# First loads one stage ahead, raw rope rows, two-pass norms and a late residual add in an eight-stage decoder layer

## The chip, the cores and the metric

The kernel runs on one core of a Trainium2 chip. The metric is the device time of one launch in microseconds (us). One execution was also taken by the hardware profiler; its times count from the start of its span.

## What is computed

One layer on 1024 tokens of width 1024, all in float32: a mixing sublayer and a retrieval sublayer, each followed by a layer norm of `alpha * x + result`.

```python
h = x @ w_in                                        # 58 blocks of 128 columns, and 12 columns "ba"
y_a = dilated_attention(rope(q_a), rope(k_a), v_a)  # 12 heads x 64, 3 patterns (window, dilation)
qkv = silu(causal_depthwise_conv(qkv_b))            # width 4
beta = sigmoid(beta_in)
g = -exp(A_log) * softplus(a_in + dt_bias)
y_b = rmsnorm(gated_delta_rule(q, k, v, g, beta)) * silu(gate_b)  # 6 heads x 128, chunks of 64
merged = gate0 * (y_a @ w_branch_attn) + gate1 * (y_b @ w_branch_delta)
x1 = layer_norm(ALPHA * x + merged @ w_out)
# PEER: 8 heads, product keys over 128 x 128 experts, top 16
s = (x1 @ w_query) against sub_keys;  experts, gate = top-k and softmax of s
act = gelu(x1 . expert_down[experts])
out = layer_norm(ALPHA * x1 + sum(gate * act * expert_up[experts]))
```

## The kernel before

The program is eight stages, one after the other, each a function with its own tiles, its own semaphores and one block of engine programs. Tile names begin with the letter of the stage:

- **p**, `stage_project` (L85): `x @ w_in`. Each of 58 weight blocks is loaded, rounded to a high part by ScalarE (ACT) and its rest taken by VectorE (DVE); TensorE (PE) multiplies high by high, high by low and low by high, so a float32 product is three matmuls (L244). The blocks come in pairs, and SyncE (SP) stores each result to `hT` in DRAM. After the last pair, 64 products of 12 columns give `psb` (L250), which goes to DRAM as `ba`.
- **a**, `stage_attention` (L255): the attention in 6 tiles of two heads. SP loads the raw q and k rows of a tile and their halves swapped (`load`, L339 and L342, 10 DMAs); POOL (GpSimd) turns them with cos and sin (L309), adds, and splits the sum into high and low parts (L313 to L316); SP copies these into the stacked operands (`restack`, L349, 12 DMAs) and the V columns (`columns`, L352). At the start PE transposes V (L495), and DVE copies it out (L445). `ahead` (L366) is SP's program for the next tile.
- **d**, `stage_deltanet` (L558): 16 chunks of the delta rule in sequence. Its start turns `ba` into beta, g and their cumulated exponentials.
- **m**, `stage_merge` (L1054): two branch products and their gates. **o**, `stage_out_norm` (L1158): the output product, 8 token tiles, each with a norm: DVE takes statistics and `(z - mean) * rstd` (L1272), POOL multiplies by the gain (L1226) and adds the bias (L1228), PE transposes the result for the next stages.
- **s**, `stage_scores` (L1348): query products. **r**, `stage_down_and_route` (L1473): 128 blocks of `x1 @ down` for 6 of the 8 token tiles, while DVE chooses experts; rows of the other two token tiles ("gathered") are fetched by POOL with indirect DMAs and multiplied on DVE.
- **e**, `stage_up` (L1946): in 32 rounds of 4 chunks, PE accumulates `C @ up` into PSUM (L2180), DVE adds each bank to `y` (L2115), prepares the low parts of the next round (L2103, L2105) and accumulates 8 gathered rows a round, `y += row * coef` (L2130), which POOL fetches (L2068). POOL also weighs the activations (L2074). At the start x1 is loaded into `y` (L2030) and taken times ALPHA. The last round brings the final norm: statistics (L1991 to L1996), `norm` (L2001) and, on POOL for all but the last tile, the gain (L2008) and the bias (L2010).

Each engine works through its own program in order and waits on semaphores. Between two stages stand barriers of all engines and the raising of the next stage's semaphores:

```python
    for s in held.values():
        nc.gpsimd.sem_inc(s, START)
    held |= {name: nc.alloc_semaphore(f"{prefix}_{name}") for name in landed.split()}
    nc.all_engine_barrier()
    yield held.__getitem__
    nc.clear_and_free_semaphores(list(held.values()))
    nc.all_engine_barrier()
```

So no load of a stage is issued before the stage ahead of it has ended on all engines and its last store has landed.

## Time and profile before

| | us |
|---|---|
| median of 3 runs | 4306.57 (4306.22 to 4308.96) |
| the profiled execution | 4310.81 |
| its span | 4309.0 |
| PE busy | 3957.7 (92% of the span) |
| DVE busy | 2586.9 (60%) |
| POOL busy | 1702.3 (40%) |
| ACT busy | 1367.3 (32%) |

The stages by their first and last matmul, and the time without a matmul ahead of each:

| stage | first and last matmul, us | no matmul ahead of it, us |
|---|---|---|
| p | 10.06 to 666.13 | |
| a | 694.99 to 965.64 | 28.9 |
| d | 985.46 to 1434.44 | 19.8 |
| m | 1449.32 to 1589.42 | 14.9 |
| o | 1603.22 to 1719.12 | 13.8 |
| s | 1729.42 to 1940.96 | 10.3 |
| r | 1959.97 to 3189.29 | 19.0 |
| e | 3208.27 to 4276.29 | 19.0 |
| end of the span | 4309.0 | 32.7 |

PE, DVE, ACT and POOL are the compute engines; SPq is SyncE issuing DMAs. The granted clock of PE is given as a share of its full speed of 2.4 GHz: 1.00 is full speed, 0.50 is 1.2 GHz. A busy time is the sum of an engine's instructions in a stretch, and what an engine waits for is inferred from the semaphores.

### The profile page before, as it was taken

The numbers are of one execution on the slowest core, as the hardware profiler recorded it, in microseconds if no ns is written. First come the engines' busy times: TensorE is split into PE (matmuls) and PEld (weight loads), VectorE is DVE, ScalarE is ACT, GpSimd is POOL, SyncE is SP. The second block draws the span as 40 slices with busy tenths as digits, with TensorE's granted clock in tenths as the row PEclk, the third lists the DMA queues.
The fourth block names the chain that finished last, engine by engine and source line by source line (L and its number), as shares of the span: only waits on it lengthen the run. The fifth ranks groups of instructions, "written<-read, shape, count | busy, mean of one in ns | idle before, by whom it ended". The sixth has DMA issues, their size and how long they took to land. (4 is left out here: it accounts for less than half of the span.)

```text
span 4309.0 us, 61280 instructions
## 1 busy us (share of the span) xinstructions
PE 3957.7 (92%) x21744; PEld 3573.4 (83%) x21744; DVE 2586.9 (60%) x5114; ACT 1367.3 (32%) x2139; POOL 1702.3 (40%) x1159
## 2 busy tenths in 40 slices
PE   9999994996888788998999999999988999999996
PEld 7888884886888666998999999999976888888885
DVE  2154102554555334116777888886648888898888
ACT  2133221652222211112472644635512222222220
POOL 0000003624444004000727656566626555555556
PEclk9999996997999899999999999999999999999998
DMA  3223224642222322223549779698888888888884
GB/s 132 97 88 106 94 86 129 160 109 71 76 75 84 138 95 94 88 68 129 136 139 318 231 227 299 201 331 278 262 315 289 289 291 290 285 290 298 280 289 185
DMA packets 390923, 801.82 MB, mean 186 GB/s; under 512 B 65265, under 2 KB 204401, under 8 KB 389745
## 3 DMA queue, kind: packets, MB, share of 16 engines
q1 hardware_dynamic: 280176, 531.25, 36.9%
q0 software_dynamic: 110592, 268.62, 19.9%
q8 instruction: 85, 1.39, 0.1%
q14 instruction: 70, 0.57, 0.0%
HBM read 623.40 MB, written 154.32 MB: 180 GB/s over the span
## 5 line engine op out<-in xcount | busy, mean ns | idle before, releaser
L1935 PE MATMUL r_psd<-x1h,r_dh 128*128 128x384 f32 x2048 | 700.9, 342 | 19.0 <-DVE r_dl L1733 19.0
L1935 PE MATMUL r_psd<-x1l,r_dh 128*128 128x384 f32 x2048 | 688.4, 336 | 0.0
L1935 PE MATMUL r_psd<-x1h,r_dl 128*128 128x384 f32 x2048 | 688.3, 336 | 0.0
L2180 PE MATMUL e_psy<-e_uh,e_Ch 128*128 128x512 f32 x1536 | 600.1, 391 | 36.3 <-DVE e_Cl L2105 31.9
L2180 PE MATMUL e_psy<-e_ul,e_Ch 128*128 128x512 f32 x1536 | 599.5, 390 | 0.0
L2180 PE MATMUL e_psy<-e_uh,e_Cl 128*128 128x512 f32 x1536 | 599.4, 390 | 0.0
L1708 POOL DMA_INDIRECT W<-r_put,r_place x256 | 426.7, 1667 | 405.6 <-DVEq L1882 319.0
L2074 POOL TENSOR_TENSOR e_araw<-e_araw,e_W 128x768 f32<-128x768 f32 x128 | 258.9, 2023 | 401.4 <-DMA e_W<-W 400.5
L1935 PEld LDWEIGHTS r_psd<-x1h,r_dh 128*128 128x128 f32 x2048 | 388.3, 190 | 19.8 <-DVE r_dl L1733 19.8
L1699 POOL DMA_INDIRECT r_rows<-in_down_rows,ids x256 | 262.7, 1026 | 358.8 <-DVE coef L1750 242.8
L2130 DVE SCALAR_TENSOR_TENSOR e_y<-e_rows,coef,e_y 128x1024 f32<-128x1024 f32 x256 | 384.5, 1503 | 15.0 <-DMA e_rows<-in_up,ids 14.9
L1935 PEld LDWEIGHTS r_psd<-x1l,r_dh 128*128 128x128 f32 x2048 | 388.3, 190 | 0.0
L1935 PEld LDWEIGHTS r_psd<-x1h,r_dl 128*128 128x128 f32 x2048 | 387.4, 189 | 0.0
L2052 ACT CAST e_uh<-e_uraw 128x1024 fp32r<-128x1024 f32 x128 | 134.8, 1053 | 789.8 <-DMA e_uraw<-in_up 495.8
L244 PE MATMUL p_ps<-p_xh,p_wh 128*128 128x512 f32 x928 | 362.0, 390 | 10.3 <-DVE p_wl L198 10.1
L2180 PEld LDWEIGHTS e_psy<-e_uh,e_Ch 128*128 128x128 f32 x1536 | 289.7, 189 | 97.8 <-DVE e_Cl L2105 32.7
L244 PE MATMUL p_ps<-p_xl,p_wh 128*128 128x512 f32 x928 | 361.6, 390 | 0.0
L244 PE MATMUL p_ps<-p_xh,p_wl 128*128 128x512 f32 x928 | 361.5, 390 | 0.0
L2068 POOL DMA_INDIRECT e_rows<-in_up,ids x256 | 331.2, 1294 | 59.1 <-issue 45.2
L2180 PEld LDWEIGHTS e_psy<-e_uh,e_Cl 128*128 128x128 f32 x1536 | 289.5, 188 | 60.5
L2180 PEld LDWEIGHTS e_psy<-e_ul,e_Ch 128*128 128x128 f32 x1536 | 289.7, 189 | 60.1
L1750 DVE CUSTOM_DVE_ANT_0 r_rows<-r_rows,r_psx 128x1024 f32<-128x1024 f32 x256 | 301.2, 1214 | 42.5 <-DMA r_rows<-in_down_rows,ids 37.1
(326 smaller groups left out, 7338.3 us busy)
## 6 DMA issues: line engine op xcount, KB each, us to landing
r_draw<-in_down SPq DMA_DIRECT2D x128, 512.0 KB, 5.3
e_uraw<-in_up SPq DMA_DIRECT2D x128, 512.0 KB, 6.2
act<-r_act SPq DMA_DIRECT2D x128, 384.0 KB, 5.0
e_araw<-act SPq DMA_DIRECT2D x128, 384.0 KB, 3.2
e_W<-W SPq DMA_DIRECT2D x128, 384.0 KB, 5.0
...
```

The lines of the kernel that those rows point to most:

```text
L244: ins = nc.tensor.matmul(ps[u][:, h * HALF:(h + 1) * HALF], a[u][:, k, :], b[:, k, h * HALF:(h + 1) * HALF], start=(k == 0 and n == 0), st ...
L1699: nc.gpsimd.indirect_dma_start(out=rows[u][:], out_offset=None, in_=g.down_rows, in_offset=bass.IndirectOffsetOnAxis(ap=g.ids[:, n, k % P: ...
L1708: nc.gpsimd.indirect_dma_start(out=cells, out_offset=bass.IndirectOffsetOnAxis(ap=place[:, n, e:e + 1], axis=0), in_=put[:, n, e:e + 1], i ...
L1750: nc.vector.tensor_tensor_reduce(out=rows[u][:], in0=rows[u][:], in1=psx[:], scale=1.0, scalar=0.0, op0=ALU.mult, op1=ALU.add, accum_out=d ...
L1935: ins = nc.tensor.matmul(psd[n][:, h, 0:HD], a[c % DEEP][:, k, :], b[:, k, h * HD:(h + 1) * HD], start=(k == 0 and m == 0), stop=(k == KD ...
L2052: nc.scalar.copy(uh[s][:], uraw[n][:]).then_inc(sem("u_hi"), 1)
L2068: nc.gpsimd.indirect_dma_start(out=rows[u][:], out_offset=None, in_=g.up.rearrange("j p d -> (j p) d"), in_offset=bass.IndirectOffsetOnAxi ...
L2074: nc.gpsimd.tensor_tensor(araw[n][:], araw[n][:], Wt[n][:], ALU.mult).then_inc(sem("weighted"), 1)
L2130: nc.vector.scalar_tensor_tensor(o, rows[u][:], scale, o, ALU.mult, ALU.add).then_inc(sem("acc"), 1)
L2180: ins = nc.tensor.matmul(bank[:], a[s][:, t * P:(t + 1) * P], v[s][:, h * HALF:(h + 1) * HALF], start=(q == 0 and m == 0), stop=(q == G - ...
```

## The change

- The semaphores of a stage are allocated and raised by POOL in the stage ahead (`raise_to_start`); between stages only the block's own end and one clear are left. Tiles that both stages see (`hand`, `out_w`, `branch_w`, `front_in`, `rope_in`, `rope_out`, `stack0`) take the first loads of the next stage, which SP issues in the stage ahead: after the last use of the buffer, and before that stage's last stores.
- In p, PE does the 12-column products after its first block product; the gate factors of d are worked out in p by ACT, DVE and PE and stay on chip. POOL turns and splits tile 0's q and k in p, and SP loads V, cos, sin, raw q and k and restacks tile 0 in p.
- In a, the sum of q or k is written over the raw rows after the high part is taken; so SP's `ahead` waits for the split, and no longer for the additions alone, before it loads the next raw rows.
- In o and e, the norm is two passes on DVE, `(z - mean) * gain` and `* rstd + bias`; POOL does the power alone. o has four weight buffers where it had two.
- In e, x1 is added late, one token tile every third round from round 3 (`add_x`); the first addition of a bank and the first two gathered rows write `y`. The first and last of the 32 rounds accumulate no rows, the second 10, the one before the last 12, the others 8 or 9. The final norm is all on DVE, and the last tile goes out in two halves.

The diff, cut to its core:

```diff
-def stage_semaphores(nc, prefix, names, landed=""):
-
-    held = {name: nc.alloc_semaphore(f"{prefix}_{name}") for name in names.split()}
-    for s in held.values():
...
+def raise_to_start(nc, sems, raised=None):
+
+    for s in sems:
         nc.gpsimd.sem_inc(s, START)
-    held |= {name: nc.alloc_semaphore(f"{prefix}_{name}") for name in landed.split()}
-    nc.all_engine_barrier()
-    yield held.__getitem__
-    nc.clear_and_free_semaphores(list(held.values()))
-    nc.all_engine_barrier()
+    if raised is not None:
+        nc.gpsimd.sem_inc(raised, 1)
 
 
...
+            table, ld_v, ld_q = g.next["ld_table"], g.next["ld_v"], g.next["ld_q"]
+            split, stacked = g.next["split"], g.next["stacked0"]
+            for i in range(att + 1, att + 17):
+                m = i - att - 1
+                pair(i)
+                if m < 6:
+                    sp.dma_start(g.vT_s[:, m, :], g.hT[2 * AT + m]).then_inc(ld_v, 16)
+                elif m < 8:
+                    sp.dma_start((g.cos_s, g.sin_s)[m - 6], (g.cos, g.sin)[m - 6]).then_inc(table, 16)
+                elif m < 12:
+                    n = m - 8
+                    block_of = g.hT[n // 2 * AT]
+                    if n % 2 == 0:
+                        sp.dma_start(g.rope_in[n][:], block_of).then_inc(ld_q, 16)
+                    else:
+                        for r in range(4):
+                            sp.dma_start(g.rope_in[n][rows[r], :], block_of[rows[r ^ 1], :]).then_inc(ld_q, 16)
+                elif m >= 14:
+                    h = m - 14
+                    sp.wait_ge(split, START + 2)
+                    for n, parts in enumerate(((0, 1), (2, 2), (3, 3))):
+                        for half, part in enumerate(parts):
+                            sp.dma_start(g.stack0[h][n][half * AD:(half + 1) * AD, :].bitcast(F32),
+                                         g.rope_out[part][h * AD:(h + 1) * AD, :].bitcast(F32)).then_inc(stacked, 16)
+            with sp.Fori(att + 17, pairs - 1) as i:
...
+            products(0, 0, first=True)
+            pe.wait_ge(ld_c, START + 96)
             for t in range(TT):
                 for k in range(KD):
                     ins = nc.tensor.matmul(psb[:, t * 2 * DH:(t + 1) * 2 * DH], x[:, k, t * P:(t + 1) * P],
                                            wba[:, k, :], start=(k == 0), stop=(k == KD - 1))
             ins.then_inc(ba_done, 1)
+            products(0, 1)
+            with pe.Fori(1, 4) as i:
+                for u in range(2):
+                    products(i, u)
+            pe.wait_ge(sem("g"), START + 1)
...
             def ahead(j, par, more=True):
 
 
+                sp.wait_ge(split, START + 4 * j + (2 * par + 4))
                 if more:
-                    sp.wait_ge(rope_done, START + 8 * j + (4 * par + 8))
                     load(2 * j + (par + 2))
-                sp.wait_ge(split, START + 4 * j + (2 * par + 4))
                 if par:
...
             ahead(AT // 2 - 1, 0, more=False)
+            for n in range(3):
+                src = g.hT[N_ATT + n * DH:N_ATT + (n + 1) * DH, :, 0:P]
+                sp.dma_start(g.front_in[n], src.rearrange("n p t -> p n t")).then_inc(g.next[f"ld_raw{n}"], 16)
             for kb in range(0, TT, 2):
...
             load_gate(0)
+            sp.wait_ge(sem("raised"), START + 1)
+            for u in range(2):
+                sp.dma_start(g.branch_w[u][:], g.w_branch[u]).then_inc(g.next[f"ld_w{u}"], 16)
+            for b in range(2):
+                sp.dma_start(g.branch_gate[:, b, :], g.hT[N_IN - N_BR + b * KD]).then_inc(g.next["ld_g0"], 16)
             sp.wait_ge(sem("none"), START + 1)
...
+            for n in range(3):
+                sp.wait_ge(sem(f"front{n}"), START + NC)
+                sp.dma_start(g.hand[n][:], g.y[n]).then_inc(g.next[f"ld_y{n}"], 16)
             sp.wait_ge(sem("y_out"), START + 2 * NC)
...
+                sp.dma_start(gates[1][:, b, :], g.hT[N_IN - N_BR + b * KD + 1]).then_inc(sem("ld_g1"), 16)
+            sp.wait_ge(sem("y_lo"), START + NK)
+            sp.wait_ge(sem("raised"), START + 1)
+            for k in range(4):
+                sp.dma_start(g.out_w[k][:], g.w_out[k * P:(k + 1) * P, :]).then_inc(g.next[f"ld_w{k}"], 16)
+            sp.dma_start(g.hand[2][:], g.x[0:P, :]).then_inc(g.next["ld_x"], 16)
             with sp.Fori(0, KD // 2 - 1) as i:
...
+                dve.wait_ge(sem("ld_c"), START + 32)
+                nc.vector.scalar_tensor_tensor(z[u][:], z[u][:], mv[:, 0:1], gain[:], ALU.subtract, ALU.mult).then_inc(sem("normed"), 1)
+                dve.wait_ge(sem("normed"), START + c + 1)
                 dve.wait_ge(sem("rstd"), START + c + 1)
-                nc.vector.tensor_scalar(z[u][:], z[u][:], mv[:, 0:1], rstd[:, 0:1], ALU.subtract, ALU.mult).then_inc(sem("normed"), 1)
+                nc.vector.scalar_tensor_tensor(z[u][:], z[u][:], rstd[:, 0:1], bias[:], ALU.mult, ALU.add).then_inc(sem("x1"), 1)
...
+            sp.wait_ge(sem("raised"), START + 1)
+            for c in (2, 0, 1):
+                if c < 2:
+                    sp.wait_ge(sem("w_lo"), START + N - 1 + c)
+                sp.dma_start(g.hand_kt[c], g.down[c]).then_inc(g.next[f"ld_d{c}"], 16)
...
+                    elif c + 2 + DEEP == PK:
+                        sp.wait_ge(sem("raised"), START + 1)
+                        sp.wait_ge(sem("st_a0"), START + 16)
+                        sp.dma_start(g.hand[2][:, 0:TD], g.act[0]).then_inc(g.next["ld_A0"], 16)
+                    else:
+                        n = (c + 2) % DEEP
+                        sp.dma_start(g.hand[n][:], g.up[n]).then_inc(g.next[f"ld_u{n}"], 16)
                 sp.wait_ge(sem("gelu"), START + c + 1)
...
-    per_round = [NU // NR] * NR
+    per_round = [0, 10] + [8] * (NR - 4) + [12, 0]
+    for n in range(NU - sum(per_round)):
+        per_round[3 + 2 * n] += 1
+    x_round = [3 + 3 * t for t in range(TT)]
...
+        def centre(dve, n):
+            dve.wait_ge(sem("stats"), START + 2 * n + 2)
+            nc.vector.bn_aggr(mv[n][:], stats[n % 2][:]).then_inc(sem("aggr"), 1)
+            dve.wait_ge(sem("aggr"), START + n + 1)
+            nc.vector.tensor_scalar(mv[n][:, 1:2], mv[n][:, 1:2], 1e-5, None, ALU.add).then_inc(sem("var"), 1)
+            dve.wait_ge(sem("ld_ln"), START + 32)
+            nc.vector.scalar_tensor_tensor(y[:, ORDER[n], :], y[:, ORDER[n], :], mv[n][:, 0:1], uraw[0][:],
+                                           ALU.subtract, ALU.mult).then_inc(sem("centred"), 1)
+
+        def finish(dve, n):
+            dve.wait_ge(sem("rstd"), START + n + 1)
+            dve.wait_ge(sem("centred"), START + n + 1)
             for h in range(2):
...
+                ins = nc.vector.scalar_tensor_tensor(half(n, h), half(n, h), rstd[n][:, 0:1], uraw[1][:, h * HALF:(h + 1) * HALF],
+                                                     ALU.mult, ALU.add)
+                if n == TT - 1:
+                    ins.then_inc(sem("final_last"), 1)
+            if n < TT - 1:
+                ins.then_inc(sem("final"), 1)
...
+            def add_x(r, t):
+
+                dve.wait_ge(sem("ld_y"), START + 16 * t + 16)
+                if t < NG2:
+                    dve.wait_ge(sem("acc"), START + first_up[r] + per_round[r])
+                else:
+                    dve.wait_ge(sem("y_add"), START + BR * r + BR)
+                o = y[:, ORDER[t], :]
+                nc.vector.scalar_tensor_tensor(o, x[:], ALPHA, o, ALU.mult, ALU.add).then_inc(sem("x_added"), 1)
...
-                        accumulate(at + done, i)
+                    add(r, b)
+                    while done < per_round[r] * (b + 1) // BR:
+                        accumulate(first_up[r] + done)
                         done += 1
-                    if prepared is not None and b % 2 == 1 and b // 2 < G:
-                        low(prepared, 1 - par, b // 2)
-
...
+                    if b % 2 == 1 and b // 2 < G:
+                        low(r + 1, 1 - r % 2, b // 2)
+                if r in x_round:
+                    add_x(r, x_round.index(r))
...
+    def held(sems, following):
+        g.sem = sems
+        after, g.ahead = stage_semaphores(nc, *following) if following else ({}, [])
+        g.next = after
+        yield after
+        nc.clear_and_free_semaphores(list(sems.values()))
```

What moves on SP at the start of attention, first in the program before: the rows are SP's instructions in order, L349 copies into the stacked operands, and a semaphore in brackets goes by the name of its first user (here `p_ld_w0` is a's `split`, and `p_ld_x7` its `rope_done`).

```order
L334 DMA a_sin<-in_sin 128x1024
L339 DMA a_raw<-hT 128x1024
L342 DMA a_raw<-hT 32x1024 x4
L339 DMA a_raw<-hT 128x1024
L342 DMA a_raw<-hT 32x1024 x4
L355 DMA a_ident<-in_ident 128x128
L357 DMA a_vT<-hT 128x1024 x6
L358 DMA a_bias<-in_bias 128x1024
L349 DMA a_stack<-a_q_hi 64x1024 [waits p_ld_w0]
L349 DMA a_stack<-a_q_lo 64x1024
L349 DMA a_stack<-a_k_hi 64x1024 x2
L349 DMA a_stack<-a_k_lo 64x1024 x2
```

In the program now:

```order
L447 UNCONDITIONAL_BRANCH [waits barrier_Pool_Activation_PE_DVE_SP_release]
L467 DMA a_bias<-in_bias 128x1024
L452 DMA hand<-hT 128x1024
L455 DMA hand<-hT 32x1024 x4
L452 DMA hand<-hT 128x1024
L455 DMA rope_in<-hT 32x1024 x4
L472 DMA later_s<-in_notlater 128x128 [waits a_raised]
L472 DMA level_s<-in_level 128x896
L472 DMA gain_s<-in_norm_gain 128x1
L465 DMA a_Vs<-a_V 128x8x128 [waits a_v_out]
```

The loads of cos, sin, the identity and V and the first restack are gone from the stage; it begins with the bias and the raw rows of tile 1.

SP in the loop over attention tiles, around the wait for the split. Before, the end of `load` and the begin of `restack`:

```order
L342 DMA a_raw<-hT 32x1024
L372 ISA
L376 ISA [waits p_ld_w0]
L349 DMA a_stack<-a_q_hi 64x1024 [waits p_w_hi]
L349 DMA a_stack<-a_q_lo 64x1024
L349 DMA a_stack<-a_k_hi 64x1024 x2
```

Now, from the loop's begin (`a_split` is the split):

```order
L492 UNCONDITIONAL_BRANCH
L492 ISA
L452 ISA [waits a_split]
L452 DMA hand<-hT 128x1024
L455 ISA
L455 DMA hand<-hT 32x1024 x2
L455 ISA
L455 DMA hand<-hT 32x1024
```

The ten load instructions stood ahead of the wait for the split (`L376`); now they stand behind it, and the restack behind them, at L462.

POOL in out_norm, before: the power, the gain and the bias of one token tile, two tiles to an iteration.

```order
L1223 REGISTER_ALU [waits p_ld_c]
L1224 TENSOR_TENSOR o_rstd<-o_mv,o_power 128x1 [waits p_x_hi]
L1226 TENSOR_TENSOR o_z<-o_z,o_gain 128x1024 [waits p_x_hi]
L1228 TENSOR_TENSOR o_z<-o_z,o_bias 128x1024 [waits p_w_hi]
L1222 REGISTER_ALU
L1224 TENSOR_TENSOR o_rstd<-o_mv,o_power 128x1 [waits p_x_hi,p_ld_c]
L1226 TENSOR_TENSOR o_z<-o_z,o_gain 128x1024 [waits p_x_hi]
L1228 TENSOR_TENSOR o_z<-o_z,o_bias 128x1024 [waits p_w_hi]
```

Now:

```order
L1300 UNCONDITIONAL_BRANCH [waits p_x_hi]
L1300 ISA
L1302 REGISTER_ALU [waits p_x_lo]
L1303 TENSOR_TENSOR o_rstd<-o_mv,o_power 128x1 [waits p_ld_x7]
L1300 REGISTER_ALU
L1300 COMPARE_AND_BRANCH
```

The two passes over 128x1024 elements are gone from POOL; DVE has two passes where it had one.

## Rows read from the trace of the kernel before

**Rows 1.** Stretches at the stages' ends: length, busy of each engine, PEclk, DMA share, GB/s.

```profile
643.30:666.10 22.80, 22.80 (x129) 22.70 (x127) 0.00 (x0) 1.02 (x1) 0.00 (x0) 0.61 0.06 24
666.10:732.00 65.90, 10.68 (x50) 6.88 (x49) 19.23 (x22) 0.00 (x0) 18.36 (x6) 0.55 0.75 200
965.60:985.40 19.80, 0.04 (x1) 0.00 (x0) 1.34 (x6) 2.70 (x3) 1.18 (x4) 0.59 0.49 146
1434.40:1449.30 14.90, 0.04 (x1) 0.02 (x1) 3.68 (x4) 2.52 (x2) 0.00 (x0) 0.50 0.62 233
1589.40:1603.20 13.80, 0.02 (x1) 0.01 (x1) 7.26 (x7) 4.08 (x4) 0.10 (x1) 0.66 0.32 115
1940.90:1960.00 19.10, 0.08 (x2) 0.03 (x1) 2.49 (x3) 2.09 (x2) 0.00 (x0) 0.62 0.57 195
3189.30:3208.30 19.00, 0.03 (x1) 0.03 (x1) 4.08 (x4) 4.48 (x6) 3.90 (x3) 0.55 0.45 159
4276.30:4309.00 32.70, 0.00 (x0) 0.00 (x0) 24.90 (x23) 0.00 (x0) 26.34 (x14) 0.56 0.27 109
```

**Rows 2.** Waits of PE: us in total, times, longest.

```profile
PE e_psy L2180 <- DVE e_Cl L2105: 31.9, 2, 19.0
PE o_ps L1320 <- DVE o_wl L1288: 21.7, 6, 13.8
PE a_psS L511 <- DMA a_Vs<-a_V: 21.1, 1, 21.1
PE o_psT L1329 <- POOL o_z L1228: 8.7, 1, 8.7
PE a_psS L511 <- DMA a_stack<-a_k_lo: 5.6, 1, 5.6
```

**Rows 3.** Timeline from the end of p: start, length, engine, instruction.

```profile
671.56 0.35 SPq L334 DMA_DIRECT2D a_cos<-in_cos  x1
686.23 3.38 POOL L309 TENSOR_TENSOR a_raw<-a_raw,a_cos 128x1024 f32<-128x1024 f32 x1 [685.79 <-DMA a_raw<-hT]
687.33 3.36 DVE L309 TENSOR_TENSOR a_raw<-a_raw,a_sin 128x1024 f32<-128x1024 f32 x1
701.41 9.45 PE L495 MATMUL a_psT<-a_ident,a_vT 128*128 128x128 f32 x42 [4.88 <-DVE a_V L445]
```

**Rows 4.** Timeline of one attention tile's supply, SP's issues and POOL's next start.

```profile
787.87 0.35 SPq L339 DMA_DIRECT2D a_raw<-hT  x1
792.89 0.48 SPq L349 DMA_DIRECT2D a_stack<-a_q_hi  x1
803.81 2.59 SPq L349 DMA_DIRECT2D a_stack<-a_k_lo  x2
812.14 2.36 POOL L313 TENSOR_TENSOR a_q<-a_raw 128x1024 f32<-128x1024 f32 x1 [3.53 <-DMA a_stack<-a_k_lo]
```

**Rows 5.** DVE by line and form in out_norm, 1640 to 1700 us: count, busy, mean ns.

```profile
L1272 DVE TENSOR_SCALAR o_z<-o_z,o_mv,o_rstd 128x1024 f32<-128x1024 f32 x6 | 4.9, 813 | 4.2 <-POOL o_rstd L1224 4.2
```

**Rows 6.** Up stage, 3425 to 4211 us, 24 rounds: DVE by line, and the stretch.

```profile
L2130 DVE SCALAR_TENSOR_TENSOR e_y<-e_rows,coef,e_y 128x1024 f32<-128x1024 f32 x194 | 299.0, 1541 | 1.8 <-DMA e_rows<-in_up,ids 1.8
L2115 DVE TENSOR_TENSOR e_y<-e_y,e_psy 128x512 f32<-128x512 f32 x290 | 195.5, 680 | 93.2 <-PE e_psy L2180 93.2
L2103 DVE TENSOR_TENSOR e_ul<-e_uraw,e_uh 128x1024 fp32r<-128x1024 f32 x96 | 116.7, 1216 | 0.0
3425.00:4211.00 786.00, 786.00 (x3469) 651.08 (x3468) 691.55 (x676) 173.71 (x192) 441.75 (x291) 1.00 0.82 290
```

**Rows 7.** The chain that ended last, its pieces in the final norm: start, length.

```profile
4259.05 1.21 DVE e_stats L1991 x2
4260.28 0.22 DVE e_mv L1994
4292.43 2.32 POOL e_y L2008
4294.81 2.67 POOL e_y L2010
```

More of the change, by code:

```diff
@@ L136, in store, with pair @@
                 sp.dma_start(g.hT[bass.ds(2 * i + u, 1)].rearrange("o p t -> (o p) t"), out[u][:]).then_inc(stored[u], 16)
-            with sp.Fori(0, pairs - 1) as i:
+            def pair(i):
                 for u in range(2):
@@ L252, in _ @@
             ins.then_inc(ba_done, 1)
+            products(0, 1)
[3 more added lines that the diff above has]
+            pe.wait_ge(sem("g"), START + 1)
+            pe.wait_ge(sem("ones"), START + 1)
+            gf = gates["g"][:].rearrange("p a b -> p (a b)")
+            nc.tensor.matmul(psg[0][:, 0:TT * DH], g.upto_s[:], gf, start=True, stop=True).then_inc(sem("G_mm"), 1)
+            nc.tensor.matmul(psg[1][:, 0:TT * DH], ones[:], gf, start=True, stop=True).then_inc(sem("G_mm"), 1)
+            with pe.Fori(4, pairs) as i:
+                for u in range(2):
+                    products(i, u)
+SEMS_A = ("a",
+    "raised ld_table ld_c ld_v ld_q v_tr v_out turned rope_done split ld_V0 ld_V1 stacked0 stacked1 s_done "
+    "masked max_ready exp_done tr_done pT_ready pv_done recip_done o_out y_tr y_out passed stored", "")
 def stage_attention(nc, g):
@@ L332, in _ @@
         def _(sp):
-            for d, s in ((cos, g.cos), (sin, g.sin)):
-                sp.dma_start(d[:], s).then_inc(ld_table, 16)
             def load(i):
@@ L672, in _ @@
         def _(pool):
-            nc.gpsimd.memset(ones[:], 1.0).then_inc(sem("ones"), 1)
+            raise_to_start(nc, g.ahead, sem("raised"))
             nc.gpsimd.memset(half_power[:], -0.5).then_inc(sem("ones"), 1)
@@ L1083, in _ @@
         def _(sp):
-            for k in range(NK):
+            for k in range(3, NK):
                 if k >= NRAW:
@@ L1112, in _ @@
                     nc.scalar.copy(wh[u][:], wraw[u][:]).then_inc(sem("w_hi"), 1)
+        @block.gpsimd
+        def _(pool):
+            raise_to_start(nc, g.ahead, sem("raised"))
         @block.vector
@@ L1410, in _ @@
             body(N // 2 - 1, last=True)
+        @block.gpsimd
+        def _(pool):
+            raise_to_start(nc, g.ahead, sem("raised"))
         @block.vector
@@ L1470 @@
 NGB = 4
+SEMS_R = ("r",
+    "raised ld_d0 ld_d1 ld_d2 ld_st ld_c ld_x st_W d_lo gelu st_a0 st_a1 st_used W d_hi shifted exp oi oj off turned rt "
+    "d_mm w_mm eq picked summed pieces passed chain zsum routed dots x_in gelu_g coef", "ld_g0 ld_g1 ld_g2 ld_g3 put0 put1")
 def stage_down_and_route(nc, g):
@@ L1690, in _ @@
         def _(pool):
+            raise_to_start(nc, g.ahead, sem("raised"))
             def gather(k):
@@ L2132, in rounds @@
-            def rounds(r, par, at, count, i=None, prepared=None, first=False):
+                dve.wait_ge(sem(f"ld_r{u}"), 16 * (k // NGU + 1))
+                if k >= NG2:
+                    dve.wait_ge(sem("acc"), START + k - NG2 + 1)
+                o, scale = y[:, GATHERED[n], :], g.coef[:, n, e:e + 1]
+                if k < NG2:
+                    ins = nc.vector.tensor_scalar(o, rows[u][:], scale, None, ALU.mult)
+                else:
+                    ins = nc.vector.scalar_tensor_tensor(o, rows[u][:], scale, o, ALU.mult, ALU.add)
@@ L2134, in rounds @@
+            for q in range(G):
+                low(0, 0, q)
+            for r in range(NR - 1):
                 done = 0
                 for b in range(BR):
[L2136 to L2138 removed]
+                    add(r, b)
+                    while done < per_round[r] * (b + 1) // BR:
+                        accumulate(first_up[r] + done)
                         done += 1
[L2140 to L2141 removed]
@@ L2143, in _ @@
-            for q in range(G):
-                low(0, 0, q)
-            dve.wait_ge(sem("ld_y"), START + 16 * TT)
-            for t in GATHERED:
-                nc.vector.tensor_scalar(y[:, t, :], y[:, t, :], ALPHA, None, ALU.mult).then_inc(sem("y_init"), 1)
-            dve.wait_ge(sem("y_init"), START + NG2)
-            rounds(0, 0, first_up[0], per_round[0], prepared=1, first=True)
-            rounds(1, 1, first_up[1], per_round[1], prepared=2)
-            with dve.Fori(1, NR // 2 - 1) as i:
-                for par in range(2):
-                    rounds(2 * i + par, par, first_up[2 + par], per_round[2], i=i, prepared=2 * i + (1 + par))
```

602 lines of the change are left out of this document (303 added, 299 removed).

## The prediction

> **What bounds the kernel now.** I read the page first: PE is busy for 92% of the span, so time can come only from the stretches in which it waits, or from an engine that takes its place. Then I read the waits of PE and the stretches at the stages' ends [rows 1, 2]. In each of these stretches PE does next to nothing, and its clock afterwards is still half for some microseconds. The timeline shows why they are long: p's last product ends at 666.1, SP issues attention's first load at 671.56, POOL starts on tile 0 at 686.23 [rows 3], and the first scores come at 732.0, after 21.1 us for V's columns and the stacked operands [rows 2]. Last I read the up stage. In its middle PE does not pause in 786.0 us while DVE is busy 691.6, 88% [rows 6], so there only PE's own work counts. At the very end 32.7 us pass without a matmul [rows 1], and their chain is POOL's gain and bias, some 5 us a token tile [rows 7].
>
> The sum is made against the profiled execution: span 4309.0, its own time 4310.81, thus 1.8 around the span. The median of the runs, 4306.57, is 4.2 lower. I take the saving off that median. A measurement of this kernel tells about 0.2% (8.6 us) from no change.
>
> **Part by part.**
>
> *Start, +0.9.* POOL raises 37 semaphores for p where it raised 26, at 0.08 us each. This is ahead of everything, so it is paid.
>
> *End of p to the first scores, -45.9.* Before, the last wide product ends at 643.6, the 12-column products take 22.8 at a clock of 0.61 on average [rows 1], and scores start at 732.0: 88.4 us. The narrow products are not removed, they move behind the first block. There they still take 22.8, and the clock falls in them; the first wide products afterwards run at half speed, for which I charge 2.2 (half speed for some 4 us). Bounds: 0 when the clock does not fall, 8 when it stays low three times as long. The last wide product then ends at 643.6 + 0.9 + 22.8 + 2.2 = 669.5. The two last stores and one barrier take 4.8 (5.4 were seen from 666.1 to the first load [rows 3]). V, cos, sin and the stacked operands of tile 0 are there already, so PE transposes V at once: 42 of the 48 transposes took 9.45 [rows 3], about 10.8 in all, and V's columns must go out and land, of which the first products no longer wait. With 1.0 for the first copy, scores start near 686.1. What hides the early work in p: DVE and ACT are far from full there, and SP's loads and copies ride on pairs of blocks of some 22 us each. If that cover is gone, the 12 copies of tile 0 and their landing come back, about 20 us.
>
> *Attention's chain, +7.2.* This speaks against the change. SP's `load` stood ahead of the wait for the split, in its shadow; now it is behind the split, and the restack behind it. In one tile [rows 4] the load is issued from 787.87, the restack from 792.89, its last issue ends at 806.4, and the data are there when POOL starts at 812.14. Split ends at 790.15 there, 2.3 after the load began. So the loop becomes: split 14.3 (six passes of 2.38), load 4.9, restack 13.5, landing 5.8, about 38 a tile where it was 36. PE's own tile takes 33.5 to 38, and waited for the stack once, 5.6 [rows 2]. From first scores to the end I get 230.9 where it was 223.7. Bounds: 0, if PE's tiles hide it, to 12, if each of five tiles pays 2.3.
>
> *Later stage ends.* The stage's end costs its last store, a barrier and a clear, some 4.4; the loads, seen to take 10 to 15 of each stretch, are gone where they sit in shared tiles. Attention to deltanet: -14.8 of 19.8, since also the gate factors are ready. Deltanet to merge: -11.7, PE at 4.4 after the end instead of 14.9, and the first block of merge no longer waits for y (1.2 more). Merge to out_norm: -16.0. Of PE's 21.7 for `o_wl` 13.8 lie in the stretch and 7.9 behind it [rows 2]; now four weight blocks are there, and the first output product is paced by DVE's 1.22 a block, ending 16.5 after the stage's begin where it took 32.5. Scores to down: -11.6 of 19.1. Down to up: -7.6 of 19.0, since W of chunk 0 can be loaded only once the last of W is written [rows 1]. Each of these could give 4 less, if a load ahead lands late.
>
> *out_norm's end and the next start, -7.7.* PE waits 8.7 for POOL's bias before the last transposes [rows 2]. On DVE, gain and bias are two passes of 1.22 (the price of a two-input pass on 128x1024 [rows 6]) in place of 0.81 [rows 5] and two POOL passes of 2.4: 2.4 less on the path. The preloaded query block gives 5.3 of the 10.3 after it. DVE's 1.6 more a tile hides beside a PE loop of 11.8.
>
> Here the Trainium skill speaks against the change: "VectorE: DVE Perf Modes", section on the perf-mode tier table, has a float32 tensor_scalar twice as fast as an operation on two tensors, so the old norm ran in a mode that the new one cannot. The trace agrees, 813 against 1216 ns [rows 5, 6]. If only that rule counted, eight final norms would cost 13 us more at the end; the POOL passes that go outweigh it.
>
> *Up stage's first rounds, -19.8.* Of the 31.9 us that PE waits for `e_Cl`, 19.0 are the stage's begin and 12.9 a stall in the second round; 4.3 more are lost ahead of that, and half speed costs about 3.7. Eight x1 loads of 512 KB are issued ahead of the second round's chunks, and cause them. They are now spread over the rounds. The 20.9 so far less 1.1 for what a first round still waits.
>
> *Rounds, 0.* Per round DVE is busy 28.8 of 32.75 [rows 6]. A ninth row adds 1.54, x1 1.3: 31.7 in the worst of 24 ordinary rounds. This is below PE's 32.75, but only just. With 12 rows, the round before the last takes 35.0 and leaves DVE 2.2 behind.
>
> *Tail, -16.4.* In the last round DVE has 12 additions at 0.60 to 0.68, 16 statistics at 0.6, 8 times 0.4 of small ones [rows 7], 8 centring passes of 1.22 and 16 half passes of about 0.68: 41. It starts some 30 ahead of PE's end, 2.2 behind: it ends about 12.7 after PE, and the store and end take 3.6, as before. 16.3 then, where 32.7 were. POOL's five us a tile (2.32 + 2.67 [rows 7]) no longer count. Bounds: 9 if statistics overlap, 24 if half passes cost like whole ones.
>
> **Sum:** 0.9 - 45.9 + 7.2 - 14.8 - 11.7 - 16.0 - 11.6 - 7.6 - 7.7 - 19.8 - 16.4 = -143.4. Span 4165.6, against the median 4306.57 - 143.4 = **4163**.
>
> **Rivals.**
>
> *A. The attention chain is hidden* and p's clock recovers at once. For it: PE waited for the stack only once. Against: slack of the later tiles was 1 to 3 us, and each tile loses 2.3. Then the time is 4163 - 7 - 2 = 4154. Chance 0.2.
>
> *B. Loads ahead come late.* They queue on SP behind waits for buffers, and share DMA with a stage's last traffic. If six stage ends give 4 less each and tile 0 of attention 12 less: 4163 + 36 = 4199. For it: one queue issues everything, at 0.45 us each and more. Against: all but two of these loads have a whole stage's last blocks to land. Chance 0.13.
>
> *C. DVE becomes the bound of the up stage; slower than before.* DVE has 1 us of room in a nine-row round. Beside a POOL pass, a DVE pass on two SBUF tensors took 3.36 instead of 1.22 [rows 3, 6]; the accumulate's mean of 1.54 contains some of it. If the shifted order made every accumulate meet POOL's weighing, 8.6 rows at +1.8 would be 15.5 a round, 13.4 beyond PE: 30 rounds, +403, giving 4566. It decides from 2.3 us an accumulate, where rounds reach 37.5 and all 143 is given back. Against: POOL's weighing, four passes of 2.0 a round, is unchanged, so at most 8 of 32.75 can collide. Chance 0.03.
>
> The Trainium skill has a rule for C: in "SBUF — State Buffer", section "SBUF: two separate sides", DVE and GpSimd share a port pair under an exclusive lock, also for a DVE operation with two SBUF inputs beside a GpSimd one that reads SBUF. The trace agrees, 3.38 on POOL and 3.36 on DVE at the same time. By that rule the tail gains when POOL falls idle, and the rounds stay as they are.
>
> *D. Waits only change their name:* the stage ends are set by the last stores and barriers, loads were hidden behind these. Against: 15 us from the first load's issue to tile 0's begin [rows 3]. Only tail, first rounds and out_norm then give, 44: 4263. Chance 0.04.
>
> **How the numbers follow.** My forecast, 4163, has 0.6, with a range of its own from 4150 to 4178 (the bounds of clock, chain and tail). A 0.2, B 0.13, C 0.03, D 0.04. The range 4143 to 4192 takes in A and the better half of B and leaves out C, D and the rest of B. Faster by over 0.2%: 0.96, the forecast, A, B and D less 0.01 that I leave within 0.2%, for a D in which DVE takes back part; slower: 0.03, which is C.
>
> **What would show it.** 17 us from the last wide product to the first scores. PE's stretches without matmuls: about 5 at deltanet, 4 to 5 at merge, 3 at out_norm, 5 at scores, 7 at down, 11 at up. First scores at 686. Attention tiles 38 apart, with PE waiting on the stack. No `e_Cl` wait inside the up stage, and PE without pause in rounds 3 to 30; the last DVE pass 13 us after PE's last matmul. The clock low for 22 to 28 us near the start of p. I am wrong if PE waits on DVE in ordinary up rounds, or if V's transposes wait for V.

## The result, and the profile after

The changed kernel takes 4249.84 us (median of 4 runs, 4245.48 to 4251.67), the kernel before beside it 4306.4. The ratio is 0.9867, 95% interval 0.985 to 0.9884: 57 us faster, where 143 were forecast. The time lies outside the range of 4143 to 4192. The profiled execution has a span of 4249.0, against 4309.0.

The page of the changed kernel, lines of parts 1 and 2:

```profile
PE 3982.7 (94%) x21744; PEld 3589.1 (84%) x21744; DVE 2557.7 (60%) x5137; ACT 1368.9 (32%) x2139; POOL 1667.6 (39%) x1134
...
PEclk8999998989999999999999999999999999999999
```

PE is busy 25 us longer than before, though it has the same 21744 matmuls. Most of the extra time is in the up stage (1074.0 us busy there, 1050.7 before), where 53.3 us of PE's work ran at a granted clock of 0.50, for 10.9 before. The stretches of the changed kernel (length, busy of PE, PEld, DVE, ACT, POOL, granted clock, DMA share, GB/s):

```profile
29.00:52.90 23.90, 23.90 (x101) 22.77 (x101) 0.26 (x1) 0.00 (x0) 0.00 (x0) 0.50 0.04 17
671.10:687.00 15.90, 10.04 (x48) 6.61 (x49) 8.50 (x16) 1.02 (x1) 0.00 (x0) 0.79 0.78 205
687.00:935.80 248.80, 222.32 (x1632) 202.78 (x1632) 129.74 (x495) 144.98 (x339) 117.15 (x50) 0.92 0.51 124
935.80:942.20 6.40, 0.04 (x1) 0.00 (x0) 0.63 (x2) 0.00 (x0) 0.00 (x0) 0.86 0.64 207
1390.40:1398.70 8.30, 0.01 (x1) 0.04 (x1) 3.85 (x5) 4.46 (x4) 0.00 (x0) 0.50 0.50 146
1534.20:1541.80 7.60, 0.01 (x1) 0.04 (x1) 6.09 (x6) 3.59 (x4) 0.10 (x1) 0.73 0.00 0
1863.90:1871.30 7.40, 0.04 (x1) 0.04 (x1) 2.55 (x3) 2.40 (x3) 0.00 (x0) 0.83 0.36 105
3098.30:3110.00 11.70, 0.02 (x1) 0.00 (x0) 3.73 (x4) 4.62 (x6) 3.70 (x3) 0.62 0.38 135
3425.00:3900.00 475.00, 445.89 (x1893) 364.92 (x1892) 369.70 (x383) 97.41 (x106) 259.19 (x166) 0.96 0.80 275
4230.20:4249.00 18.80, 0.00 (x0) 0.00 (x0) 14.41 (x25) 0.00 (x0) 4.54 (x3) 0.61 0.27 109
```

Against [rows 1]: the stretches at the ends of a, d, m, s and r fell from 19.8, 14.9, 13.8, 19.1 and 19.0 us to 6.4, 8.3, 7.6, 7.4 and 11.7. The last wide product of p ends at 671.1, and scores start 15.9 us behind it. The middle of the up stage, which had no pause [rows 6], now has PE busy for 445.89 of 475 us, at a clock of 0.96. The account by stage, from the first and last matmuls of both traces:

| part | before | after | difference | forecast |
|---|---|---|---|---|
| begin to first scores | 732.0 | 687.0 | -45.0 | -45.0 |
| attention from its first scores | 233.6 | 248.8 | +15.2 | +7.2 |
| a to d, with deltanet | 468.8 | 454.5 | -14.3 | -14.8 |
| d to m, with merge | 155.0 | 143.8 | -11.2 | -11.7 |
| m to o, out_norm, o to s | 140.0 | 117.7 | -22.3 | -23.7 |
| s, s to r, r | 1459.9 | 1446.5 | -13.4 | -11.6 |
| r to e | 19.0 | 11.7 | -7.3 | -7.6 |
| **up stage** | **1068.0** | **1120.1** | **+52.1** | **-19.8** |
| tail | 32.7 | 18.8 | -13.9 | -16.4 |

Seven parts came within 2.5 us. Attention missed by 8, and the up stage by 72, most of the whole miss. PE's longest waits in the changed kernel (us in total, times, longest):

```profile
PE e_psy L2276 <- DVE e_Cl L2199: 57.8, 15, 11.7
...
PE a_psS L616 <- DMA a_stack<-rope_out: 10.3, 2, 9.8
...
PE a_psS L616 <- DMA stack<-rope_out: 7.3, 2, 5.1
...
PE o_psT L1407 <- DVE xgl L1354: 6.6, 1, 6.6
```

57.8 us for DVE's low parts in 15 waits, where 31.9 in 2 were [rows 2]: 11.7 lie ahead of the stage, 46.1 in it. They come in a pattern. From first matmul to first matmul, rounds 0 to 2 take 38.4, 34.4 and 32.6 us, rounds 3 to 23 between 34.1 and 39.0, rounds 24 to 29 again 32.6. Rounds 3, 5, ..., 21 are those with nine rows, and PE waits between every one of these ten and the round behind it: 1.5 to 6.1 us, some 39 of the 46.1. The other four waits stand ahead of rounds 1, 9, 23 and 31. What DVE and POOL wait for, 3170 to 3940 us of the changed kernel:

```profile
DVE e_y L2222 <- DMA e_rows<-in_up,ids: 140.4, 51, 6.6
```

```profile
POOL hand L2172 <- DMA e_W<-W: 252.6, 42, 8.1
POOL e_araw L2172 <- DMA e_W<-W: 55.3, 13, 7.4
```

DVE is not short of time: it stands 140.4 us and waits for gathered rows. One such wait in the timeline (start, length, engine, instruction; SP, POOL and DVE each in an answer of its own):

```profile
3554.99 0.43 SPq L2117 DMA_DIRECT2D e_W<-W  x1
```

```profile
3551.46 1.95 POOL L2166 DMA_INDIRECT e_rows<-in_up,ids  x1 [0.31 <-issue]
3561.54 1.85 POOL L2172 TENSOR_TENSOR hand<-hand,e_W 128x768 f32<-128x768 f32 x1 [8.13 <-DMA e_W<-W]
3563.54 0.97 POOL L2166 DMA_INDIRECT e_rows<-in_up,ids  x1
3564.81 0.95 POOL L2166 DMA_INDIRECT e_rows<-in_up,ids  x1 [0.31 <-issue]
```

```profile
3553.64 0.95 DVE L2199 TENSOR_TENSOR e_Cl<-hand,e_Ch 128x768 fp32r<-128x768 f32 x1
...
3568.13 1.28 DVE L2222 SCALAR_TENSOR_TENSOR e_y<-e_rows,coef,e_y 128x1024 f32<-128x1024 f32 x1 [5.86 <-DMA e_rows<-in_up,ids]
3569.34 1.22 DVE L2197 TENSOR_TENSOR e_ul<-hand,e_uh 128x1024 fp32r<-128x1024 f32 x1
```

DVE makes a low part at 3553.64; that lets SP load the block of W two chunks on, at 3554.99. POOL ended a gather at 3553.4 and then stood 8.13 us in front of the weighing that needs this block. The next row's gather starts at 3563.54 behind it, and this is the row that DVE waits 5.86 us for (the semaphores of both agree). DVE takes it at 3568.13, and only at 3569.34 goes on with the low parts that SP's next load, and PE a round later, need. That such delays add up until PE itself stops (next for 3.6 us at 3610.5) is argued from this order, not read from one line.

### The profile page after: what moved, and what is told of

Read it like the earlier page. It is cut to its first block and busy times, and to the rows that moved or that the text cites. A ratio compares the mean times of both kernels' runs of the same rounds, so it can differ in the third digit from the quotient of the medians.

```text
span 4249.0 us, 59296 instructions
## 1 busy us (share of the span) xinstructions
PE 3982.7 (94%) x21744; PEld 3589.1 (84%) x21744; DVE 2557.7 (60%) x5137; ACT 1368.9 (32%) x2139; POOL 1667.6 (39%) x1134
## 3 DMA queue, kind: packets, MB, share of 16 engines
q8 instruction: 86, 1.41, 0.1%
## 5 line engine op out<-in xcount | busy, mean ns | idle before, releaser
L2276 PE MATMUL e_psy<-e_uh,e_Ch 128*128 128x512 f32 x1536 | 610.2, 397 | 57.8 <-DVE e_Cl L2199 57.8
L2222 DVE SCALAR_TENSOR_TENSOR e_y<-e_rows,coef,e_y 128x1024 f32<-128x1024 f32 x254 | 361.2, 1422 | 171.3 <-DMA e_rows<-in_up,ids 163.6
L2150 ACT CAST e_uh<-hand 128x1024 fp32r<-128x1024 f32 x128 | 134.7, 1052 | 802.0 <-DMA hand<-in_up 718.9
L2166 POOL DMA_INDIRECT e_rows<-in_up,ids x256 | 340.5, 1330 | 59.6 <-issue 51.0
L274 DVE TENSOR_TENSOR p_wl<-p_wraw,p_wh 128x1024 fp32r<-128x1024 f32 x58 | 73.6, 1268 | 358.9 <-ACT p_wh L199 358.8
```

The source lines that it names most:

```text
L274: nc.vector.tensor_tensor(wl[u][:], wraw[u][:], wh[u][:].bitcast(F32), ALU.subtract).then_inc(w_lo, 1)
L2150: nc.scalar.copy(uh[s][:], uraw[n][:]).then_inc(sem("u_hi"), 1)
L2166: nc.gpsimd.indirect_dma_start(out=rows[u][:], out_offset=None, in_=g.up.rearrange("j p d -> (j p) d"), in_offset=bass.IndirectOffsetOnAxi ...
L2222: ins = nc.vector.scalar_tensor_tensor(o, rows[u][:], scale, o, ALU.mult, ALU.add)
L2276: ins = nc.tensor.matmul(bank[:], a[s][:, t * P:(t + 1) * P], v[s][:, h * HALF:(h + 1) * HALF], start=(q == 0 and m == 0), stop=(q == G - ...
```

## Theories

**G, late gathers.** A circle: DVE's accumulate waits for a row; POOL fetches the row behind a weighing in program order; the weighing waits for W; SP loads W once DVE has made the low parts two chunks back; these stand behind the accumulate on DVE. With 8 rows a round the circle had slack: DVE waited 1.8 us for rows in 24 rounds [rows 6]. POOL's four steps of a round split nine rows as 2, 2, 2, 3, where the ninth row is the first to be fetched. So each of the first three steps leaves one of the next round's rows to the step behind it.

**C**, the prediction's rival: DVE has too much work in nine-row rounds. **X:** x1's late loads and passes are at fault.

**L**, for attention: the load behind the split stretches each tile's supply.

## Experiments

### Gathers rounded to the earlier step

```diff
-  for k in range(first_up[r] + per_round[r] * q // G, first_up[r] + per_round[r] * (q + 1) // G):
+  for k in range(first_up[r] - -per_round[r] * q // G, first_up[r] - -per_round[r] * (q + 1) // G):
```

This kernel is `e_ceil`.

> Up stage only: POOL's gathers of an uneven round are rounded up to the earlier chunk steps (9 rows: 3, 2, 2, 2 in place of 2, 2, 2, 3); DVE and PE do exactly the same work. Theory G (late gathers: in and after a nine-row round the rows are fetched one chunk step later, behind a weighing that waits for W, whose load waits for DVE, which waits for the rows): the up stage falls from 1120 us to about 1060, PE's waits in rounds 3 to 24 nearly vanish, the time goes from 4250 to about 4190. Rival C (DVE has too much work in a nine-row round): no change, 4250 within 5. Rival X (the late x1 load and pass): no change.

4203.88 us (4199.77 to 4219.26), ratio to before 0.9761 (0.9733 to 0.9789). The stage takes 1080.2 us with 22.9 of waits inside. The order of gathers alone, with DVE's work unchanged, gives back 40 us of the up stage. C alone and X alone are out. But 20 us more than G's 1060 are left: rounds of 33 to 38 us remain, and G as stated is not complete.

### Without x1

The eight loads and eight passes of `add_x` are taken out; this leaves x1 out of the final norm's input (`e_nox`).

> Leaves out x1 in the up stage: no load of x1 and no pass that adds it, eight of each. Theory G: the stage stays above 1105 us of 1120 (eight passes of 1.2 us and eight loads less). Rival X (x1's load or pass makes the stalls): the stage falls to about 1060. Rival C: DVE loses 1.2 us of some 31 in every third round, the stage falls by up to 10.

One run: 4245.17 us, the stage 1116.2 for 1120.1, with 44.9 of waits inside. X falls. The 4 us less say nothing: in the three kernels below that leave the up stage as it is, the stage took 1117.0, 1118.6 and 1109.8.

### Eight rows in every round

```diff
-    per_round = [0, 10] + [8] * (NR - 4) + [12, 0]
+    per_round = [8] * (NR - 2) + [16, 0]
```

The first eight gathers go back beside the weighings of chunks 4 to 7 (`e_rows8`).

> Up stage: 8 rows in each of rounds 0 to 29, 16 in round 30, 0 in round 31; the first eight gathers issued beside the last weighings of the start, as in the kernel before. x1 stays late. Theory G and rival C: no stalls in rounds 3 to 29, the stage near 1060 us; DVE enters the last round about 8 us late, which the tail pays: 19 becomes up to 27, time about 4195 to 4200. A theory of shared DMA bandwidth or of x1: stalls stay, 1100 or more.

One run: 4206.01 us, the stage 1072.7. Rounds 2 to 29 all take 32.6 us. The forecast missed the cost of the end by some 12: round 30, with 16 rows, takes 47.1, since PE waits 14.3 there, and the first round, with rows again, 41.7 for 38.4.

### Extra work on DVE in odd rounds

```diff
+  if b in (5, 9) and r % 2 == 1 and 3 <= r <= 21:
+      ...
+      nc.vector.tensor_tensor(spent[:], y[:, DENSE[0], 0:896], y[:, DENSE[1], 0:896], ALU.add).then_inc(sem("extra"), 1)
```

on top of the eight rows (`e_work2`; the waits in front of the addition are left out here).

> As e_rows8 (8 rows a round, no stalls), and in each odd round from 3 to 21 DVE does two additions of 128x896 more, some 1.07 us each, more than the ninth row's 1.28; their result isn't used. Theory G (the stalls come from late gathers, DVE has room): rounds stay at 32.6, at most 33. Rival C (2.1 us more work on DVE are enough for the stalls): odd rounds or those after them take 34 to 37 us, the stage grows by 20 or more over e_rows8's 1072.7.

One run: 4205.92 us. The same stretch of the middle, first of the eight rows, then with the extra work:

```profile
3425.00:3900.00 475.00, 475.00 (x2098) 393.43 (x2097) 425.02 (x415) 104.03 (x116) 267.54 (x174) 1.00 0.83 295
```

```profile
3425.00:3900.00 475.00, 475.00 (x2098) 393.46 (x2097) 420.08 (x430) 106.39 (x116) 292.46 (x173) 1.00 0.84 294
```

PE is busy for all 475 us in both, and every round from 2 to 29 takes 32.6. The additions fit, and they cost more than was thought: 14 of them in the stretch took 1.55 us each, not 1.07. Yet DVE's busy time fell by 5 us. Its other passes got shorter, the low parts of C in `hand` from 1.72 to 1.06 us and the accumulates from 1.53 to 1.41, presumably because the extra passes moved them against POOL's; this is not shown. So the run shows that extra passes do not bring the stalls, but not that DVE has room for 2.1 us more in all; that is left to the next experiment. A row also differs from an addition in that it must be fetched.

### Gathers ahead of the weighing

```diff
-                    if r + 2 < NR:
-                        weigh(G * (r + 2) + q)
                     for k in range(first_up[r] + per_round[r] * q // G, first_up[r] + per_round[r] * (q + 1) // G):
                         if k + NGU < NU:
                             gather(k + NGU)
+                    if r + 2 < NR:
+                        weigh(G * (r + 2) + q)
```

This kernel is `e_gfirst`.

> The changed kernel, with the gathers of a POOL step ahead of its weighing, and the steps rounded down as there (2, 2, 2, 3 in a nine-row round). Theory G: with the gather ahead of the weighing that waits, the rounding matters little: stage 1060 to 1075. Rival C: 1105 or more, as in the changed kernel.

One run: 4178.57 us, the stage 1051.8, better than the 1060 to 1075 forecast. With both edits, the order and the rounding (`e_gfirst_ceil`):

> As e_ceil, and POOL issues a step's gathers ahead of its weighing, not behind it; DVE and PE do the same work. Theory G in full (also what e_ceil left, 22.9 us of PE waits and nine-row rounds of 34 to 36 us, comes from gathers that queue behind the weighing): the up stage falls from 1080 us to about 1058, nine-row rounds to 32.6 to 33, the time from 4204 to about 4182. Rival C for the rest (what is left is DVE's work in nine-row rounds): no further change, 4204 within 5.

4178.57 us (4176.76 to 4181.88), ratio to before 0.9706 (0.9687 to 0.9726). The stage takes 1051.7, all rounds from 2 on 32.6 to 32.8. PE's, then DVE's waits (3170 to 3940), then the stretch:

```profile
PE e_psy L2276 <- DVE e_Cl L2199: 15.3, 2, 11.6
```

```profile
DVE e_y L2209 <- PE e_psy L2276: 90.0, 83, 2.0
```

```profile
3425.00:3900.00 475.00, 475.00 (x2097) 393.31 (x2096) 414.52 (x420) 106.70 (x118) 300.69 (x185) 1.00 0.85 305
```

Of the 57.8 us of PE's waits 15.3 are left, 11.6 of them ahead of the stage, and DVE now waits for PE and not for rows. C falls by `e_gfirst`: DVE has the passes of the changed kernel there, nine-row rounds included, its accumulates take even more of its time (392.3 us for 361.2 over the stage), and PE does not pause from round 1 on. G holds, in a wider form: it is the gather's place behind the waiting weighing that made the nine-row rounds slow, and the rounding matters no more once the order is mended. The changed kernel's stage was 68 us longer. Waits inside are 46.1 against 3.6, 42.5 of it. The other 26 are PE's busy time (1120.1 - 46.1 = 1074.0 against 1048.1). The granted clock fell to half around most of the waits, as the 0.96 of the stretch shows where [rows 6] have 1.00: 53.3 us of PE's work in the stage ran at half, for 6.5 here, and half of that difference, 23.4 us, is what the clock cost.

### The sum of q and k in a tile of its own

The tile `a_qk` takes the float32 sum, and the wait changes place:

```diff
-                sp.wait_ge(split, START + 4 * j + (2 * par + 4))
                 if more:
+                    sp.wait_ge(rope_done, START + 4 * (2 * j + par + 2))
                     load(2 * j + (par + 2))
+                sp.wait_ge(split, START + 4 * j + (2 * par + 4))
```

This kernel is `a_qk`; the rest is the changed kernel's.

> Attention only: the float32 sum of q or k goes to a tile of its own, so SP loads the next raw rows after the additions, ahead of the wait for the split, as in the kernel before. Theory L (load behind the split lengthens each tile's supply chain): from first scores to attention's last matmul 248.8 us becomes 235 to 241 (233.6 before). Rival: the chain is longer for another reason (loads ahead for deltanet, the first restack), it stays at 246 or more.

One run: 4232.32 us; from first scores to attention's end 239.0 us. L holds: about 10 of the 15 us. One tile's supply in the changed kernel, SP and then POOL, to be read beside [rows 4]:

```profile
751.14 0.36 SPq L452 DMA_DIRECT2D hand<-hT  x1
756.19 13.54 SPq L462 DMA_DIRECT2D stack<-rope_out  x12
```

```profile
748.57 2.38 POOL L432 TENSOR_TENSOR rope_out<-hand,rope_out 128x1024 fp32r<-128x1024 f32 x1
775.20 2.38 POOL L429 TENSOR_TENSOR rope_out<-hand 128x1024 fp32r<-128x1024 f32 x1 [3.56 <-DMA stack<-rope_out]
```

and with the tile of its own:

```profile
746.72 0.36 SPq L454 DMA_DIRECT2D hand<-hT  x1
752.38 13.89 SPq L464 DMA_DIRECT2D stack<-rope_out  x12
```

```profile
746.62 2.40 POOL L434 TENSOR_TENSOR rope_out<-a_qk,rope_out 128x1024 fp32r<-128x1024 f32 x1
769.88 2.36 POOL L431 TENSOR_TENSOR a_qk<-hand 128x1024 f32<-128x1024 f32 x1 [2.46 <-DMA stack<-rope_out]
```

From one split's begin to the next it is 38.5 us in the one (736.67 to 775.20) and 35.4 in the other (734.52 to 769.88). Of what is left against before (239.0 for 233.6), the first stack that comes out of the stage, tile 1's, is the likely part: PE waits 8.9 us for it.

### Both mended

`e_gfirst` and `a_qk` together are `gfirst_qk`.

> e_gfirst and a_qk together. They touch different stages, so the gains should add: attention at 250 us where it is 260.6, the up stage at 1052, the time 4178.6 - 10 = 4168.6.

4170.26 us (4165.15 to 4175.3), ratio to before 0.9673 (0.9658 to 0.9688). Attention's stage takes 251.1 us from its first transpose, the up stage 1052.2. The two gains add within the spread of the runs.

### Tile 1's raw rows loaded in the project stage too

```diff
+                    if h == 1:
+                        for n in range(0, 4, 2):
+                            block_of = g.hT[1 + n // 2 * AT]
+                            sp.dma_start(g.rope_in[n][:], block_of).then_inc(ld_q, 16)
+                            for r in range(4):
+                                sp.dma_start(g.rope_in[n + 1][rows[r], :], block_of[rows[r ^ 1], :]).then_inc(ld_q, 16)
...
-            load(1)
```

On top of both, this is `gfirst_qk_load1`.

> gfirst_qk, and the raw q and k rows of tile 1 are loaded in the project stage too, after tile 0's restack. In a_qk POOL starts on tile 1 at 688.9, 15 us after attention's first load is issued, and PE then waits 8.9 us for tile 1's stack; with the rows there at 674 the stack lands near 722, as PE ends tile 0. Theory L in full (attention is paced by this chain): attention 250.6 falls to 236 to 241, the time to 4154 to 4159. Rival (PE's own tile or V's columns pace it): 246 or more, 4164 or more.

4167.02 us (4156.64 to 4168.52, 5 runs), ratio to before 0.9665 (0.9652 to 0.9678). By the medians this is 3 us below the kernel ahead of it and within the spread of both, so no gain in the whole time is shown. It is also above the 4154 to 4159 of the expectation, where the rival had it. The profiled execution was the fastest of the five. Its attention takes 241.6 us from the first transpose for 251.1, just outside the 236 to 241 of the expectation. From the first scores it is 230.4, now less than the 233.6 of before, so in this one profile the first tile's wait was what was left. POOL's begin on tile 1, and PE's wait for the stack:

```profile
681.88 7.00 POOL L432 TENSOR_TENSOR hand<-hand,spare 128x1024 f32<-128x1024 f32 x3 [130.79 <-issue]
```

```profile
PE a_psS L624 <- DMA stack<-rope_out: 2.6, 1, 2.6
PE a_psS L624 <- DMA a_stack<-rope_out: 0.9, 1, 0.9
```

The rows were there, yet POOL began 5.4 us after the stage did (676.5): it raises deltanet's 62 semaphores first, at 0.08 us each, the last at 681.7. The long wait for tile 1 is gone.

### out_norm's norm as before

Back in out_norm alone: `(z - mean) * rstd` on DVE in one pass, gain and bias on POOL (`o_pool`).

> out_norm alone gets the norm of the kernel before: one pass on DVE, gain and bias on POOL. Theory (two DVE passes of 1.22 replace 0.81 and two POOL passes of 2.4 on the last tile's path): the wait before the last transposes rises from 6.6 us to 8.7 to 9.5, out_norm from 105.1 to 107 to 108, the loop of its tiles stays bound by PE. Rival (DVE's extra pass slows the tile loop, so that the old norm is better): 103 or less.

One run: 4244.48 us. PE's wait ahead of the last transposes:

```profile
PE o_psT L1410 <- POOL o_z L1309: 8.7, 1, 8.7
```

8.7 us where the two-pass norm has 6.6, and the stage takes 107.2 for 105.1 (104.9 to 105.1 in every other kernel with the two passes). The two passes on DVE win 2.1 us there, near the 2.4 worked out. The whole time can't tell: the up stage alone took between 1109.8 and 1120.1 in four profiles of the same code.

### One boundary without its loads ahead

out_norm no longer loads the two query blocks; the score stage does so at its begin (`s_noahead`).

> One boundary gets its first loads back into its own stage: the two query weight blocks of the score stage are loaded when it begins, as in the kernel before; the short way between stages stays. If the loads ahead carry the gain, the stretch without a matmul ahead of the scores rises from 5.0 us by 4 to 6 (10.3 before), and out_norm stays at 105. If the removed barriers and semaphore raises carry it, the stretch rises by 1 to 2.

One run: 4237.45 us. The stretch ahead of the scores, in the changed kernel and then in this one:

```profile
1646.90:1651.90 5.00, 0.04 (x2) 0.03 (x1) 2.53 (x3) 3.00 (x3) 0.00 (x0) 0.50 0.10 11
```

```profile
1643.00:1651.80 8.80, 0.13 (x2) 0.04 (x1) 2.51 (x3) 3.10 (x3) 0.00 (x0) 0.50 0.57 173
```

From last to first matmul it is 8.7 us where it was 5.0, and 10.3 before. The loads ahead carry 3.7 us at this boundary and the shorter way between stages 1.6: a little under the 4 to 6 forecast, and more than the 1 to 2 of the other theory. The whole time is lower than the changed kernel's all the same, since the up stage was shorter in this run (1109.8 for 1120.1); nothing follows from it. The other boundaries were not tried by themselves, so how their gains divide is not shown.

## Why the prediction was wrong, point by point

- **Begin to first scores: right, and its exactness is luck.** -45.0 measured, -45.0 forecast. But the working takes the 0.9 of the start twice: 669.5 holds it, 686.1 - 732.0 is -45.9 with it, and the sum adds 0.9 again. Without that slip this term is -45.9 and the sum -144.3. First scores came at 687.0 for 686.1. The narrow products' half-speed stretch is there, 23.9 us at 0.50 near the start of p.
- **Stage ends: each sum within 2.5 us, in part by luck.** Ahead of merge 8.3 us pass for the 4 to 5 foretold, and merge itself is 4.6 shorter. Ahead of out_norm it is 7.6 for 3; from merge's last matmul to the end of the first output product the kernel saves 14.8 for the 16.0. The gains are real, but two stretches were 4 us longer than thought, and shorter insides hid it.
- **out_norm: right**, and o_pool shows the 2.1 us by itself. What the Trainium skill says in "VectorE: DVE Perf Modes", on the tier table, held for the direction of DVE's price and did not decide, as the prediction weighed it. The trace has 1216 against 813 ns, a ratio of 1.5 and not the 2 of the prediction's words.
- **Attention's chain: right in mechanism, mis-sized.** +7.2 forecast, +15.2 measured; a_qk takes 9.8 of it back. The working speaks of 223.7 us before, where the trace has 233.6; only the difference went into the sum. A tile costs 38.5 as worked out (38). What the term left out is the first tile that the stage itself must feed, tile 1. Its raw rows are issued 11.4 us ahead of the first scores, where it was 15.5 before. So POOL begins on it 1.5 us behind the first scores, where it began 1.6 ahead, and PE waits 9.8 us for its stack. The bound of 12 was too low as well.
- **Up stage's first rounds: near.** Rounds 0 and 1 take 72.8 where they took 88.6, -15.8 for -19.8. PE still waits 3.3 us ahead of round 1, for the 1.1 allowed, and its granted clock falls to 0.50 there once, for 3.4 us.
- **"Rounds, 0": the step that failed.** It read "A ninth row adds 1.54 ... This is below PE's 32.75, but only just", and looked at DVE's busy time alone. DVE's time was enough: with the gathers ahead, the same passes on DVE leave PE without a pause from round 1 on (e_gfirst). What I did not follow was the fetch of the ninth row: on POOL's queue it stands behind a weighing that waits for a load that waits for DVE. The cost is 68 us against the mended order (1120.1 against 1051.7), 42.5 of waits and 26 of PE's busy time, 23 of these by the clock. Without it the stage would have stood at 1051.7 against the 1048.2 forecast. The prediction's own sign of being wrong, "if PE waits on DVE in ordinary up rounds", is what the trace shows.
- **Tail: right within 2.5 us** (18.8 for 16.3). DVE's passes cost what was taken. The last tile's end in the changed kernel's timeline, centring, POOL's power, and the two half passes:

```profile
4242.16 1.27 DVE L2099 SCALAR_TENSOR_TENSOR e_y<-e_y,e_mv,hand 128x1024 f32<-128x1024 f32 x1
4242.32 1.51 POOL L2190 TENSOR_TENSOR e_rstd<-e_mv,e_power 128x1 f32<-128x1 f32 x1 [3.95 <-DVE e_mv L2097]
4243.87 1.42 DVE L2106 SCALAR_TENSOR_TENSOR e_y<-e_y,e_rstd,hand 128x512 f32<-128x512 f32 x2 [0.43 <-POOL e_rstd L2190]
```

The power takes 1.51 us beside DVE's pass, where its piece of the chain before was 0.51, and DVE waits 0.43 for it. DVE ends 15.1 us after PE, for the 12.7 of the sum (its own terms, 41 less 30 and 2.2 behind, make 13.2).
- **The rivals.** A failed: the chain is not hidden, and the clock in p did not recover at once (the narrow products end at 47.8, the half level at 52.9). B holds in places: attention's tile 1 came late, which cost PE 9.8 us, and the stretches ahead of merge and out_norm are 4 longer than foretold. It failed as a whole: with the stages behind them, the ends gave their sums within 1.4 us. C named the right place and the wrong cause, and its price was for another event. D failed. None of the rivals was the circle of waits; a chance for a stall in uneven rounds was missing, and the range was thus too narrow.

With the gathers' order mended the change gives 4178.6 us, with attention's load mended too 4170.3, both inside the range that the unmended one missed.

## What to carry to other kernels

A change of how many items a round takes is not costed by the busy engine alone: follow the fetch of the extra item back through every program order that it stands in, and ask what each instruction ahead of it waits for. Here a prefetch had to stand ahead of the waiting instruction on its queue, not behind it; look for that order first. A tile that is reused to save memory moves a wait: see what was in that wait's shadow.

## What the runs showed beyond the question

PE's short waits in the up stage (14 of at most 6.1 us, 46.1 in all) cost more than half as much again. Against the mended order, 42.5 us more of waiting came with 26 us more of busy time, 0.6 for each, and 23.4 of these are work at half clock. Not every wait brought it: behind the 2.6 us ahead of 3395.3 and the 1.2 ahead of 3429.4 the granted clock stayed at 1.00.

A batch of ten small loads at a stage's begin is slow to be of use. SP issued tile 1's in 4.7 us (675.6 to 680.3), and POOL began only at 688.54, 8.3 us behind the last issue. The kernel before had the same: 8.8 for tile 0 and 7.7 for tile 1, and 4.8 to 6.7 for the four tiles behind them. Why the first batches take longer is not shown.
